# VectorE's low half of a head pair's attention output, moved one pair later in VectorE's program

## The reference, cut to what matters

```
q = rope(q); k = rope(k)
s = q . k * 64**-0.5, masked; m = max(max(s), sink)
p = exp(s - m); p = p / (sum(p) + exp(sink - m))
o = p @ v
```

## Time and profile before

| what | value |
|---|---|
| median of 3 runs | 1743.88 us (1743.76 to 1744.52) |
| the profiled execution's own time | 1743.15 us |
| its span, first to last instruction | 1741.2 us |
| mean granted TensorE clock | 0.989 |
| TensorE busy | 97% of the span |
| VectorE, ScalarE, GpSimd busy | 71%, 42%, 49% |
| window attention, first to last scores (line 692) | about 98.5 to 194 us |

### The profile page before, as it was taken

One profiled execution on the slowest core, in us unless ns is written; L12 is line 12 of the kernel. 1 busy time (PEld: TensorE's weight loads), 2 busy tenths in 40 slices (PEclk: granted clock), 3 DMA queues, 4 the chain that ended last, 5 costly groups with the idle time before them and its releaser, 6 DMA issues.

```text
span 1741.2 us, 26658 instructions
## 1 busy us (share of the span) xinstructions
PE 1682.2 (97%) x9077; PEld 1481.1 (85%) x9077; DVE 1229.3 (71%) x2262; ACT 734.2 (42%) x1102; POOL 856.5 (49%) x573
## 2 busy tenths in 40 slices
PE   6988999999999999999899999998999999999997
PEld 5766788888878899999899999997888888888886
DVE  6576522212146699999699999733888888888888
ACT  5467642222242233333366666532333333333333
POOL 7531134444433368998777777784323322333320
PEclk9999999999999999999999999999999999999999
DMA  6211112222322248989779999999999999999993
GB/s 245 91 52 49 38 61 97 97 96 96 109 73 85 85 147 296 325 299 315 256 265 354 335 349 356 332 381 330 402 354 360 378 361 348 378 361 345 377 361 122
DMA packets 127107, 424.80 MB, mean 244 GB/s; under 512 B 13264, under 2 KB 29648, under 8 KB 124880
## 3 DMA queue, kind: packets, MB, share of 16 engines
q1 hardware_dynamic: 80688, 264.28, 42.5%
q0 software_dynamic: 36864, 134.23, 20.9%
q10 hardware_dynamic: 9504, 25.71, 3.7%
HBM read 371.74 MB, written 52.43 MB: 244 GB/s over the span
## 4 chain that ended last, share of the span: by engine, by line
PE 79%; DVE 14%; DMA 2%; DVEq 1%; ACT 1%; issue 1%; SPq 0%; POOL 0%; ACTq 0%
PE bank L865 30%; PE both L512 11%; PE bank L523 11%; PE bank L512 9%; PE bank L527 5%; PE both L621 3%; PE bank L848 3%; DVE rows L1435 2%; PE bank L765 2%; DVE chosen L1517 2%; DVE cand L1459 1%; DMA raw<-stream 1%; DVE chosen L1511 1%; PE both L645 1%; DMA subkeys<-subkeys 1%
## 5 line engine op out<-in xcount | busy, mean ns | idle before, releaser
L465 POOL TENSOR_TENSOR w_lo<-raw,w_hi 128x1024 fp32r<-128x1024 f32 (+1 forms) x302 | 553.5, 1844 | 468.9 <-ACT w_hi L913 467.8
L913 ACT ACTIVATE w_hi<-raw 128x1024 fp32r<-128x1024 f32 x346 | 367.1, 1061 | 854.7 <-PE bank L865 316.8
L486 POOL DMA_INDIRECT rows<-stream,idx x256 | 299.1, 1168 | 371.8 <-DVE both L1623 308.8
L523 PE MATMUL bank<-hT_hi,w_hi 128*128 128x384 f32 x1024 | 348.2, 340 | 5.2 <-ACT abuf L1116 5.2
L523 PE MATMUL bank<-hT_lo,w_hi 128*128 128x384 f32 x1024 | 343.4, 335 | 0.0
L865 PE MATMUL bank<-w_hi,wT_hi 128*128 128x512 f32 x768 | 196.4, 391 | 6.6 <-ACT wT_hi L1155 6.6
L527 PE MATMUL bank<-hT_hi,w_lo 128*128 128x384 f32 x1024 | 198.4, 334 | 0.8 <-POOL w_lo L465 0.8
L523 PEld LDWEIGHTS bank<-hT_hi,w_hi 128*128 128x128 f32 x1024 | 193.3, 189 | 5.8 <-issue 4.8
L865 PE MATMUL bank<-w_hi,wT_lo 128*128 128x512 f32 x768 | 195.9, 390 | 0.0
L865 PE MATMUL bank<-w_lo,wT_hi 128*128 128x512 f32 x768 | 195.2, 389 | 0.0
L1608 DVE TENSOR_TENSOR w_lo<-raw,w_hi 128x1024 fp32r<-128x1024 f32 x128 | 156.8, 1225 | 53.5 <-ACT w_hi L913 52.8
(11 more groups left out here) (268 smaller groups left out, 2447.2 us busy)
## 6 DMA issues: line engine op xcount, KB each, us to landing
raw<-stream SPq DMA_DIRECT2D x346, 512.0 KB
a_rows<-abuf ACTq DMA_DIRECT2D x64, 384.0 KB
g_rows<-gstage SPq DMA_DIRECT2D x32, 768.0 KB
g_in<-g_rows SPq DMA_DIRECT2D x16, 1536.0 KB
a_in<-a_rows SPq DMA_DIRECT2D x64, 384.0 KB, 6.2
rows<-stream,idx POOLq DMA_INDIRECT x256
x_sb<-x SPq DMA_DIRECT2D x4, 512.0 KB, 8.4
out<-x_sb SPq DMA_DIRECT2D x4, 512.0 KB, 3.0
```

Source lines behind the costliest of these rows:

```text
L465: last = pool.tensor_tensor(w_lo[:, k % 2, cols], raw[:, k % RAW, cols], w_hi[:, k % 2, cols].bitcast(f32), ALU.subtract)
L486: pool.indirect_dma_start(rows[:, g % SLOTS, :], None, table, bass.IndirectOffsetOnAxis(idx[:, g // HK, g % HK:g % HK + 1], 0)).then_inc(g ...
L523: pe.matmul(dst, w_hi[:, slot, k * P:(k + 1) * P], hT[low][:, k, DENSE], start=(k == 0 and low == 0), stop=False)
L913: act.activation(w_hi[:, base % 2, :], raw[:, slot, :], ACT.Copy).then_inc(hi_ready, 1)
```

## The change

In window attention VectorE no longer makes the low half of pair u - 1's output at the end of its pass for pair u. It makes it in the pass for pair u + 1, behind the maxima, `negm`, `sdiff` and the rotation of that pass, and ahead of the normalising. Pairs 6 and 7 are taken over by the first two passes of memory attention, each behind `negm`; heads 0 and 1 of memory attention get their low half behind `negm` of passes 2 and 3, and heads 2 and 3 theirs at the end. TensorE's, ScalarE's, GpSimd's and SyncE's programs, and all waits of theirs, are as they were. The instructions are the same ones in the same number.

```
                 if u < 7:
                     dve.wait_ge(proj_read, R_Q + u + 2)
                     rotate(*turned_q, bank_done=True)
+                if u >= 2:
+                    outputs_low(8 + u - 2, 4 + u - 1)
                 for j in range(2):
                     cols = slice(4 * j, 4 * j + 4)
                     dve.wait_ge(expd, 2 * u + j + 1)
...
                         last.then_inc(prob_ready, 1)
-                if u >= 1:
-                    outputs_low(8 + u - 1, 4 + u)
...
                 dve.tensor_scalar(negm[:, 0:TT], mx[:, 0:TT], -(P ** -0.5), None, ALU.mult).then_inc(capped, 1)
-                if u == 0:
-                    outputs_low(8 + 7, 12)
+                if u < 2:
+                    outputs_low(8 + 6 + u, 11 + u)
+                else:
+                    outputs_low(4 + u - 2, 12 + u - 1)
                 dve.wait_ge(score_read, 32 + 4 * (u + 1))
...
                                      ALU.mult).then_inc(prob_ready, 1)
-                if u >= 1:
-                    outputs_low(4 + u - 1, 12 + u)
-            outputs_low(4 + 3, 16)
+            for u in (3, 4):
+                outputs_low(4 + u - 1, 12 + u)
```

## The result

| | before | changed |
|---|---|---|
| median of five runs each | 1743.76 us (1742.46 to 1744.52) | 1750.08 us (1748.91 to 1752.64) |
| ratio, 95% interval | | 1.0045 (1.0033 to 1.0056) |
| span of the profiled execution | 1741.2 us | 1748.1 us |
| window attention, first to last score product (line 692) | 98.5 to 192.1 us | 97.8 to 200.1 us |

The medians differ by 6.3 us. The ratio is estimated from all runs and is not the quotient of the two medians; by it the change costs 0.45%. A second session gave 1749.24 against 1742.47 us, 1.0050 (1.0036 to 1.0063). The forecast was 1752.3 us, slower than before.

A forecast was written before the change was run, and what follows sets the result against it. TensorE, busy 97% of the span, was taken to bound the kernel. Stalls +5.5, clock +3.1 and memory attention -0.2 gave +8.4 us on 1743.15: 1751.5, with 0.7 for the median 1752.3 us; range 1745.5 to 1761.

The forecast's parts named there:

- What the stall of before was: Before line 621, the query projection: `outputs_low` delays `rotate_bank`; removing this takes away five stalls, -9.0 us.
- The new wait: At line 645, the value blocks, TensorE waits 2.9 us for `yT_lo` in five passes: 14.5 instead of 9.0, +5.5 us.
- `sdiff` slips through: On VectorE, `sdiff`, asked for right behind a waiting `negm`, loses no turn to GpSimd; `negm` and `sdiff` go to 128.55.
- rival 1: On VectorE behind `negm`, `sdiff` loses a turn to GpSimd as well: stall about 3.85 us, total 1759 us; chance 0.16.
- Rival 3: `negm` and rotation do not collide with GpSimd: stall 1.55 to 1.85 us, -2.3 us, total 1741.5 us; chance 0.16.
- The clock: TensorE behind the 2.9 us stalls: three half-speed stretches in five passes against one before, +3.1 us.
- the bound of 2.1 us: TensorE's wait length from which half speed, clock 0.50, becomes possible behind it: 2.1 us.
- Memory attention: Normalising for head 0 no longer stands behind pair 7's low half; TensorE waited only 0.2 us there: -0.2 us.
- The sum: Whole run: 5.5 + 3.1 - 0.2 = +8.4 us on the profiled execution's 1743.15 us.
- One to one behind 256 us: Behind 256 us TensorE runs without waits to the expert stages, so the whole delay carries through.

The follow-up runs named there:

- the best version: Changed kernel with the moved `outputs_low` put right behind `rotate_bank` and GpSimd's low halves in eight pieces instead of four: 1729.14 against 1741.51 us before, 0.9928.

## Why the prediction was right, step by step

- **What the stall of before was** (`rotate_bank` held up by `outputs_low`): right, and closer than forecast. In the changed kernel it ends at 125.34, 0.02 us before TensorE has done its transposes and not 0.3, because the maxima begin 1.2 us behind the scores instead of 0.94. The 9.0 us before line 621 are gone but for 0.07 us in each of the five passes.
- **The new wait**: right in place and nearly in size. Stalls of 2.8 to 3.1 us were expected, and 2.9 taken; four are 3.04 us and one 3.08. `negm` took 0.69 us, because it asked just after GpSimd's second piece had begun and not in the first one as I had laid it out, and the rotation 1.22 and 1.10 us. GpSimd's bursts took 3.25 us, a little under the forecast "over 3.3". The five waits came to 15.2 instead of 14.5 us. A sixth of about 0.4 us, in the pass without rotation, I had put at nothing: there too `negm` waits for GpSimd (0.59 us).
- **`sdiff` slips through** (rival 1): right, 0.15 us behind each waiting `negm`, with four pieces, with one, and in the best version with eight. It lost its turn only where `negm` had not waited: 0.46 us with eight pieces in the changed kernel, 0.71 us in one pass with the low half behind `rotate_bank`, and 0.75 us at 104.96 in the earlier trace rows. Rival 1 would have given 3.85 us a stall.
- **Rival 3** (no collision, 1741.5 us) is what the run with `w_hi` later measures: stalls of 1.6 us, no half speed, 0.15% faster than before. Its price was right; its condition, no collision, does not hold in the changed kernel.
- **The clock**: over-sized. I took three half-speed stretches in place of one, +3.1 us; there were two, in both profiles of the changed kernel. Each costs 16.15 - 14.54 = 1.6 us, so the term is 2 x 1.6 - 1.56 = +1.7. The number of stretches was a guess, and the bound of 2.1 us, read from two waits, does not hold in other runs: half speed followed waits of 2.0 us with eight pieces and with one.
- **Memory attention**: right, -0.2 us.
- **The sum**: from the first projection behind the 2.9 us wait (112.44, before 113.12) to the projection behind memory attention's first transposes (223.59, before 215.65) the time grew by 8.6 us. Of that the terms give 6.2 + 0.4 + 1.7 - 0.2 = 8.1, and the five times 0.07 us before line 621 another 0.4. That it lies so near the forecast 8.4 is in part luck: the clock term was 1.4 us too large, and the stalls, the sixth wait and the 0.07 us together 1.5 us too small.
- **"One to one behind 256 us"**: not quite. The output projection starts 8.0 us later (460.1 against 452.1), the end of the span is 6.9 us later. About 1 us came back in the expert stages. The stretches at half speed lie differently there in each profile, and I did not separate that from anything else. Another 0.7 us are no effect of the change: in this profile the first score product, ahead of anything that was moved, starts at 97.8 instead of 98.5 us, and over all profiles with four or eight pieces it starts between 97.4 and 99.0. These two, and not the size of the stage, bring the profiled 6.9 us, and the medians' 6.3, under my 8.4.

## What to carry to other kernels

Moving a short instruction off one wait puts it behind others: work out the time at which its result is next asked for, and place it as the last thing that is still ready by then, but no later (places between `rotate_bank` and `sdiff` were not tried). Here 2.3 us of rotation between "behind `sdiff`" and "behind the rotation" separate 0.47% faster from 0.45% slower. Before moving VectorE work whose operands all lie in SBUF, look at what GpSimd does in its new place: the two engines wait for each other's whole instructions, even an instruction on eight columns with a single operand, and cutting GpSimd's work into smaller pieces bounds that wait. The turns are not fixed by the program: which instruction waits depends on where its start falls between the pieces, so expect the forecast of one instruction to be off by a piece.

## What the runs showed of the hardware

- An 8-column `negm` of 0.17 us took 0.69 us beside GpSimd pieces of 0.73 us, 0.37 beside pieces half as wide, and 1.63 and up to 2.21 beside one of 2.37 us. `outputs_low`, with one operand in PSUM, kept its 0.68 us in the middle of a burst.
- GpSimd pays too: its bursts grew from 2.83 to 3.25 us with four pieces, and to 4.29 to 4.34 with eight, which without a collision take 3.38.
- Of five equal stalls of 3.0 us two were followed by half speed, those that ended at 146 and 177 us, in both sessions; three were not. Of the five waits of 2.0 us with eight pieces one was, and an early wait of 2.75 us in two runs was not. The length of a stall alone does not decide it.
